# Norms split over three engines, a reordered head, a store in parts, and a quarter of the gate rows on ScalarE, in a two-layer kernel

## The chip, the cores and the metric
The kernel runs on one core of a Trainium2 chip. The metric is the device time of one execution in microseconds; the median of the runs is compared. Five engines matter here: TensorE (PE in the rows; PEld is its weight load), VectorE (DVE), ScalarE (ACT), GpSimd (POOL) and SyncE (SP), whose queue issues most of the DMAs.

## The reference, cut to what matters
Two transformer-like layers over 256 tokens of width 1024, everything in float32. Layer one:

```python
mod = silu(c) @ w_ada + b_ada                    # 6 x 1024 values: shift, scale, gate, twice
xn = rms_norm(h, norm1_g) * (1.0 + sc1) + sh1
proj = xn @ w_in                                 # q, k, v of 8 heads; RWKV inputs; gate logits
mixed = g_moba * (attention @ w_proj_moba) + g_rwkv * (rwkv @ w_proj_rwkv)
h = h + gt1 * (mixed @ w_out)
xn2 = rms_norm(h, norm2_g) * (1.0 + sc2) + sh2
h = h + gt2 * peer_ffn(xn2, ...)                 # q = xn2 @ wq, top 16 of 16384 experts per head
```

`rms_norm` is x * rsqrt(mean(x*x) + eps) * gain over the 1024 features. `peer_ffn` chooses for each token and each of 8 heads 16 of 128 x 128 experts, takes gelu(xn2 . u) times the softmaxed score, and sums the experts' v rows. The second layer is of the same shape: norm, `w_in_2`, two attentions, `w_o`; then norm, `w_up`, a causal convolution of width 3, silu gate, `w_down`:

```python
x = x + gate_a * ((g_a * o_a + g_b * o_b) @ w_o)
h = rms_norm_2(x, ffn_norm) * (1.0 + scale_f) + shift_f
x = x + gate_f * ((silu(gt) * val) @ w_down)
```

So there are four norms over the residual, each between two matrix products.

## The kernel before, in words
Activations lie transposed: 128 partitions hold features, and a tile `hT[:, m, :]` is 128 features of all 256 tokens; the residual is 8 such tiles. Weights come as tiles of 128 x 1024 (512 KB) through a ring `wring` of six slots. SyncE issues them in order, each as soon as the tile six earlier is done (`tile_done`). Most products are computed in three TensorE passes of a split: ScalarE writes the rounded upper part of a tile to `whi` (L455, three slots), VectorE the rest to `wlo` (L460), and `three` (L463) multiplies upper by upper, upper by rest and rest by upper. The phases "w_in", "wq", "peer", "w_in2" and "ffn" are split so; "proj", "w_out" and "w_o" multiply float32 directly, and each such float32 matmul stands in the trace as two records.

Each engine has its own list of work, written out by hand at the end of the kernel (from L2329); semaphores alone tie them together. There is no planner.

The norm (L503 to L537) is a relay in which each step handles all eight tiles: `norm_squares` (VectorE, one operation on 2048 columns), `norm_pe` (eight matmuls with ones into bank 3), `norm_act` (square root on ScalarE), `norm_scale` (reciprocal, and the product of all tiles with it, VectorE), `norm_shift` (eight operations on VectorE with the modulation's scale and shift), `x_upper` (eight casts on ScalarE) and `x_rest` (four subtractions on VectorE). TensorE begins when all of `xn` is there (L835, L1813) or all of the split (L1451, L2200).

The head: SyncE loads the silu input `crow`, four tiles of `ada` (512 KB each), then columns, constants, x and positions, then twelve more `ada` tiles, each waiting for a free slot of four, then six weight tiles. VectorE forms one dot product per `ada` tile (L822, 128 x 1024); sixteen are needed for the first norm: eight scales and eight shifts. TensorE computes the first four tiles of w_in, the values with tokens on partitions, one tile after another: for each tile and token half eight matmuls with 128 columns (`matmul8_tokens`, L488). After that come the split tiles, beside which VectorE runs eight more dot products, and the position angles (`dve_trig`, L896) run ahead of all splits.

The gate rows (`dve_hot` L1584, `pe_gates` L1600, `act_gates` L1613): for 64 groups of four tokens VectorE builds one-hot rows, A4 (one operation for four tokens, L1589) and B4 (one operation per token, one-hot times the gate weight, L1591); TensorE multiplies them, four tokens into one bank, and one matmul of an early expert tile stands between groups (L1611); ScalarE copies the bank to `G` and, once in eight groups, takes the Gelu of an early expert tile.

After the experts the sum lies with tokens on partitions; TensorE turns it back (L1687) and VectorE adds it to the residual (L1794). At the end `dve_add_accs` (L1801) waits for the last tile, adds all eight accumulators, and SyncE stores the result with one DMA (L2323).

Of the kernel before, what the change touches and what calls it, by code (L numbers as in the profile page):

```python
# [15 lines left out]
P = 128  # L16
# [154 lines left out]
def build_layer_pair(nc, a):  # L171

    with ExitStack() as ctx:
# [65 lines left out]
        aring = rA["aring"].rearrange("p (s n) -> p s n", s=ASLOTS)  # L239
        zraw = arena[:, 3584:3584 + 14 * 257].rearrange("p (m t) -> p m t", m=14)  # L240
# [25 lines left out]
        rB, _ = region(arena, 32256, [("crow", D), ("aring", BSLOTS * D)])  # L266
# [6 lines left out]
        rG, _ = region(arena, S * NK + 2 * KT * S, [("T3", 768), ("A4", 1024), ("B4", 1024)])  # L273
        rG.update(region(arena, AFTER_WHI, [("ge", 768), ("crow2", D), ("iota", 128)])[0])
        rG.update(region(arena, AFTER_WHI + 768, [("iotai", 128)])[0])
# [98 lines left out]
        def ring_tiles(pe, name, body):  # L374
# [23 lines left out]
            for k in range(n, count):  # L398
                one(slot_of(first + k), (ring0 + k) % BANKS, count_at(first + k), ring0 + k - BANKS + 1)

# [102 lines left out]
        def norm_pe(pe, n, sq):  # L503
            pe.wait_ge(sq_ready, n + 1)
            for k in range(KT):
                mm = pe.matmul(bank[3][:, 0:S], ones, sq[:, k, :], start=(k == 0), stop=(k == KT - 1))
            mm.then_inc(ss_ready, 1)

        def norm_act(act, n, rt):
            act.wait_ge(ss_ready, n + 1)  # L510
            act.activation(rt, bank[3][:, 0:S], ACT.Sqrt, scale=1.0 / D, bias=col("eps")).then_inc(rt_ready, 1)

        def norm_squares(dve, sq):
            dve.tensor_tensor(sq[:, :, :], hT[:, :, :], hT[:, :, :], ALU.mult).then_inc(sq_ready, 1)

        def norm_scale(dve, v, n, rt):
            dve.wait_ge(rt_ready, n + 1)
            v.then(dve.reciprocal(rt, rt))
            v.then(dve.tensor_tensor(xn[:, :, :], hT[:, :, :], over(rt, KT), ALU.mult))

        def norm_shift(dve, n, shift):
# [4 lines left out]
        def x_upper(act, n):  # L526

            for k in range(KT):
                act.wait_ge(xn_ready, KT * n + k + 1)
                act.copy(xhi[:, k, :], xn[:, k, :]).then_inc(x_hi, 1)  # L530

        def x_rest(eng, n):

            for k in range(0, KT, 2):
                eng.wait_ge(x_hi, KT * n + k + 2)
                eng.tensor_tensor(xlo[:, k:k + 2, :], xn[:, k:k + 2, :], xboth[:, k:k + 2, 0, :].bitcast(F32),
                                  ALU.subtract).then_inc(x_lo, 1)  # L537

# [160 lines left out]
        def sp_loads(sp):  # L699
            for dst, src in ((cols[:, :], a["cols"]), (keep[:, :], a["keep"]), (hT[:, :, :], a["xT"]),  # L700
                             (posi, a["positions"].to_broadcast([P, S]))):
                sp.dma_start(dst, src).then_inc(loaded, 16)

        def sp_ada(sp):

            sp.dma_start(crow, a["crow"][0:1, :].to_broadcast([P, D])).then_inc(crow_loaded, 16)
            for t in range(2 * KT):
                if t == ASLOTS:
                    sp_loads(sp)
                if t >= ASLOTS:  # L710
                    sp.wait_ge(ada_used, t - ASLOTS + 1)
                sp.dma_start(aring[:, t % ASLOTS, :], a["ada"][t]).then_inc(alanded[t % ASLOTS], 16)

        def sp_w_in(sp):
# [9 lines left out]
            for t in range(SLOTS):  # L724
                sp.dma_start(wring[:, t, :], a["w"][t]).then_inc(landed[t], 16)
            sp.dma_start(r0["const1"], a["const1"][:, 0:NC1]).then_inc(c1_loaded, 16)
            sp.dma_start(rA["select1"], a["const1"][:, NC1:NC1 + NS1]).then_inc(c1_loaded, 16)
# [8 lines left out]
        dots_before = lambda j: min(max(3 * j // 2, 0), 3 * KT)  # L736
# [81 lines left out]
        def dve_ada(dve, n):  # L818

            dve.wait_ge(alanded[n % ASLOTS], 16 * (n // ASLOTS + 1))  # L820
            src = aring[:, n % ASLOTS, :]
            dve.tensor_tensor_reduce(src, src, crow, 1.0, 0.0, ALU.mult, ALU.add, mod[:, n:n + 1]).then_inc(ada_used, 1)  # L822

# [10 lines left out]
        def pe_w_in(pe):  # L834
            pe.wait_ge(xn_ready, KT)  # L835
# [21 lines left out]
        def act_w_in_tile(act, t):  # L857

            if t + 2 >= SKIP["w_in"]:
                act_hi_of(act, "w_in", t + 2)  # L860
            tile_wait(act, "w_in", t)
            bk = bank[t % BANKS]
            if t < 4:
# [1679 lines left out]
```

## Time and profile before

| what | us |
|---|---|
| median of 3 runs | 1910.35 (1909.63 to 1910.8) |
| profiled execution | 1909.39 |
| its span, first to last instruction | 1907.6 |
| TensorE busy | 1731.3 (91%) |
| VectorE busy | 1337.7 (70%) |
| ScalarE busy | 728.6 (38%) |
| GpSimd busy | 98.9 (5%) |
| granted TensorE clock, mean | 0.962 of full |
| chain of waits: TensorE, VectorE | 77%, 17% |

Busy time is the union of an engine's instructions. The chain of waits is followed back from the last instruction; a share in it is time on which the end depends. 316 MB move, 166 GB/s as a mean over the span.

### The profile page before, as it was taken

To read this page: it belongs to the slowest core of one execution; us is meant where nothing else is said; L and a number is where in the kernel's file an instruction comes from. 1 tells how busy PE (TensorE), PEld (TensorE's weight loads), DVE (VectorE), ACT (ScalarE), POOL (GpSimd) and SP (SyncE) were. 2 spreads that over 40 slices of the span, in tenths; PEclk is the share of its full clock that TensorE was granted. 3 is DMA by queue.
4 is the path that set the end of the run, shared out by engine and by line. 5 is a ranking of instruction groups with operands and counts; after the bars stand their busy time and mean duration, and the time that the engine had idled before them with its cause. 6 is when DMAs were issued, how large, how long until landed. Compare 5 with 4: busy or idle time off the path is not lost.

```text
span 1907.6 us, 30181 instructions
## 1 busy us (share of the span) xinstructions
PE 1731.3 (91%) x10370; PEld 1503.9 (79%) x10370; DVE 1337.7 (70%) x2720; ACT 728.6 (38%) x1275; POOL 98.9 (5%) x107
## 2 busy tenths in 40 slices
PE   2987999969997989999999999999799988879997
PEld 2986888759885767788888888887798846669997
DVE  7678553763999977688888888887445545448886
ACT  1443101113212344455555555554244215324443
POOL 0022000000000000000000000000007103200000
PEclk8999999989998989999999999999899988989999
DMA  9642003655561127677777777777355460035553
GB/s 332 233 136 69 23 16 108 216 216 165 159 189 46 56 81 242 211 234 240 233 237 235 236 239 234 239 234 222 110 181 152 125 209 1 23 96 180 182 181 110
DMA packets 101311, 316.24 MB, mean 166 GB/s; under 512 B 11248, under 2 KB 20464, under 8 KB 100720
## 3 DMA queue, kind: packets, MB, share of 16 engines
q1 hardware_dynamic: 100512, 311.07, 51.2%
q10 hardware_dynamic: 720, 4.11, 0.6%
q8 instruction: 50, 0.82, 0.2%
q14 instruction: 29, 0.24, 0.0%
HBM read 309.63 MB, written 5.51 MB: 165 GB/s over the span
## 4 chain that ended last, share of the span: by engine, by line
PE 77%; DVE 17%; DMA 2%; issue 2%; POOL 1%; ACT 1%; SPq 0%; ACTq 0%; DVEq 0%; POOLq 0%
PE bank L481 8%; PE bank L466 7%; PE bank L467 7%; PE bank L468 7%; PE bank L1647 6%; PE bank L1649 6%; PE bank L1651 6%; PE bank L482 4%; PE bank L1606 4%; PE bank L442 3%; PE bank L492 2%; PE bank L1398 2%; PE bank L582 1%; PE bank L1496 1%; PE bank L485 1%
## 5 line engine op out<-in xcount | busy, mean ns | idle before, releaser
L460 DVE TENSOR_TENSOR wlo<-wring,whi 128x1024 fp32r<-128x1024 f32 x348 | 423.9, 1224 | 114.5 <-ACT whi L455 106.7
L455 ACT CAST whi<-wring 128x1024 fp32r<-128x1024 f32 x364 | 380.9, 1048 | 73.5 <-PE bank L1651 49.1
L466 PE MATMUL bank<-xboth,whi 128*128 128x256 f32 x960 | 276.3, 288 | 25.5 <-DVE wlo L460 23.3
L467 PE MATMUL bank<-xboth,whi 128*128 128x256 f32 x960 | 273.3, 285 | 0.0
L468 PE MATMUL bank<-xboth,wlo 128*128 128x256 f32 x960 | 273.2, 285 | 0.0
L481 PE MATMUL bank<-xboth,whi 128*128 128x512 f32 x658 | 235.8, 397 | 0.0
L466 PEld LDWEIGHTS bank<-xboth,whi 128*128 128x128 f32 x960 | 186.0, 194 | 28.9 <-issue 24.4
L467 PEld LDWEIGHTS bank<-xboth,whi 128*128 128x128 f32 x960 | 186.1, 194 | 0.6 <-issue 0.5
L468 PEld LDWEIGHTS bank<-xboth,wlo 128*128 128x128 f32 x960 | 185.9, 194 | 0.0
L482 PE MATMUL bank<-xboth,wlo 128*128 128x256 f32 x658 | 184.5, 280 | 0.0
L1647 PE MATMUL bank<-whi,Whi 128*128 128x512 f32 x512 | 161.0, 396 | 14.9 <-DVE Wlo L1742 14.9
L1649 PE MATMUL bank<-wlo,Whi 128*128 128x512 f32 x512 | 159.9, 394 | 0.0
L1651 PE MATMUL bank<-whi,Wlo 128*128 128x512 f32 x512 | 159.0, 392 | 0.0
L481 PEld LDWEIGHTS bank<-xboth,whi 128*128 128x128 f32 x658 | 123.6, 188 | 29.4
L1496 PE MATMUL bank<-xn,wring 128*128 128x256 f32 x544 | 128.6, 380 | 0.0
L482 PEld LDWEIGHTS bank<-xboth,wlo 128*128 128x128 f32 x658 | 124.2, 189 | 3.7
L1647 PEld LDWEIGHTS bank<-whi,Whi 128*128 128x128 f32 x512 | 97.3, 191 | 33.4 <-issue 9.8
L1649 PEld LDWEIGHTS bank<-wlo,Whi 128*128 128x128 f32 x512 | 97.2, 190 | 21.5
L1651 PEld LDWEIGHTS bank<-whi,Wlo 128*128 128x128 f32 x512 | 97.0, 189 | 21.4
L1496 PEld LDWEIGHTS bank<-xn,wring 128*128 128x128 f32 x544 | 98.6, 191 | 10.7
L1751 DVE TENSOR_TENSOR arena<-arena 128x256 f32<-128x256 f32 x94 | 59.8, 636 | 56.0 <-ACT arena L1710 56.0
L460 POOL TENSOR_TENSOR wlo<-wring,whi 128x1024 fp32r<-128x1024 f32 x16 | 45.7, 2862 | 1016.4 <-ACT whi L455 1016.4
(367 smaller groups left out, 2893.5 us busy)
## 6 DMA issues: line engine op xcount, KB each, us to landing
wring<-in_w SPq DMA_DIRECT2D x463, 512.0 KB, 3.9
arena<-in_ada SPq DMA_DIRECT2D x48, 512.0 KB, 5.6
xn<-in_ada SPq DMA_DIRECT2D x96, 256.0 KB, 3.3
h_spill<-arena SPq DMA_DIRECT2D x34, 128.0 KB, 1.7
arena<-h_spill SPq DMA_DIRECT2D x34, 128.0 KB, 3.5
wring<-in_w SPq DMA_DIRECT2D x6, 384.0 KB, 3.1
wring<-in_w SPq DMA_DIRECT2D x9, 256.0 KB, 2.6
arena<-in_const ACTq DMA_DIRECT2D x1, 1200.0 KB, 5.3
```

What stands on the lines that cost most here:

```text
L455: act.copy(whi[:, n % HSLOTS, :], wring[:, n % SLOTS, :]).then_inc(hi_ready, 1)
L460: eng.tensor_tensor(wlo[:, n % SLOTS, :], wring[:, n % SLOTS, :], whi[:, n % HSLOTS, :].bitcast(F32), ALU.subtract).then_inc(lo_ready, 1)
L466: pe.matmul(out, h, xh, start=start, stop=False, **kw)
L467: pe.matmul(out, h, xl, start=False, stop=False, **kw)
L468: return pe.matmul(out, l, xh, start=False, stop=stop, **kw)
L481: pe.matmul(out, h, xboth[:, k, :, :], start=(k == 0), stop=False)
L482: pe.matmul(out[:, 0:S], l, xhi[:, k, :], start=False, stop=False)
L1496: mm = pe.matmul(bank[j % 3][:, 0:S], blocks(n % SLOTS, k), xn[:, k, :], start=(k == 0), stop=(k == KT - 1))
L1606: mm = pe.matmul(bank[3 + n % 4][:, t * 128:(t + 1) * 128], A4[:, n % 2, t, :], B4[:, n % 2, t, :], start=True, stop=True)
L1647: pe.matmul(tok_accs[b][f][:, :], Wh, h[:, f * 512:(f + 1) * 512], start=first, stop=False)
L1649: pe.matmul(tok_accs[b][f][:, :], Wh, l[:, f * 512:(f + 1) * 512], start=False, stop=False)
L1651: mm = pe.matmul(tok_accs[b][f][:, :], Wl, h[:, f * 512:(f + 1) * 512], start=False, stop=last)
```

## The change
1. Norms. Squares go to ScalarE, a tile at a time; the ones-matmul of a tile follows in TensorE's list two tiles behind the product that made it (in w_out and w_o). The sum lies in bank 4. After the reciprocal VectorE scales tile by tile, ScalarE shifts (Identity with scale and bias from columns) and casts, and VectorE subtracts pairs of tiles. TensorE waits for rows or pairs of rows: `split_pair` runs the first two weight tiles of wq and of ffn together, over k outside. Those two tiles are split before the norm ends (beside the residual).
2. Head. A ring of sixteen slots; scale and shift tiles come in pairs of the same feature tile; SyncE issues everything without waiting, weight tiles among them. The four value tiles are computed together, k outside, 512 columns a matmul. The angles' operations stand between the splits of tiles 6, 7 and 8.
3. Dot products beside proj and w_out are spread by a table (DOTS). `crow` of that stage lies elsewhere.
4. Gate rows. VectorE builds three of the four B4 rows; ScalarE the fourth, as Relu(gate - gate * (id - iota)^2), in two operations.
5. End. The last down tile signals each pair of accumulators; adds and store follow in four parts.
6. Semaphores of the head norms of the attentions are merged into one family (`head_*`), with counts carried on; nothing in the order of those operations changes.

```diff
+        hring = arena[:, 7680:7680 + 2 * KT * D].rearrange("p (t n) -> p t n", t=2 * KT)
...
-        def matmul8_tokens(pe, bk, slot, width=128):
+        def matmul8_tokens(pe, bk, slot, norm=None, width=128):
             for b in range(TT):
                 for k in range(KT):
+                    if norm is not None and b == 0:
+                        pe.wait_ge(xn_ready, KT * norm + k + 1)
...
+        def act_square(act, n, m, sq):
+            act.activation(sq[:, m, :], hT[:, m, :], ACT.Square).then_inc(sq_ready, 1)
+        def norm_sum(pe, n, m, sq):
+            pe.wait_ge(sq_ready, KT * n + m + 1)
+            mm = pe.matmul(bank[NORM_BANK][:, 0:S], ones, sq[:, m, :], start=(m == 0), stop=(m == KT - 1))
...
+        def norm_scale(dve, rt):
             for k in range(KT):
-                dve.tensor_scalar(xn[:, k, :], xn[:, k, :], gsc[:, n, k:k + 1], modc(shift, k),
-                                  ALU.mult, ALU.add).then_inc(xn_ready, 1)
+                dve.tensor_tensor(xn[:, k, :], hT[:, k, :], rt, ALU.mult).then_inc(x_scaled, 1)
+        def norm_shift(act, n, k, shift):
+            act.wait_ge(x_scaled, KT * n + k + 1)
+            act.activation(xn[:, k, :], xn[:, k, :], ACT.Identity, scale=gsc[:, n, k:k + 1],
+                           bias=modc(shift, k)).then_inc(xn_ready, 1)
...
+        def norm_shift_split(act, n, shift):
+            norm_shift(act, n, 0, shift)
+            for k in range(1, KT):
+                norm_shift(act, n, k, shift)
+                x_upper(act, n, k - 1)
+            x_upper(act, n, KT - 1)
...
+        def split_pair(pe, outs, n, norm):
+            for k in range(KT):
+                if k % 2 == 0:
+                    pe.wait_ge(x_lo, 4 * norm + k // 2 + 1)
+                for i in range(2):
+                    mm = three(pe, outs[i], n + i, k, xhi[:, k, :], xlo[:, k, :], k == 0 and (i == 0 or outs[2]),
+                               k == KT - 1, skip_group_check=True)
...
+            sp.dma_start(crow, a["crow"][0:1, :].to_broadcast([P, D])).then_inc(crow_loaded, 16)
+            pair(0)
+            for dst, src in ((hT[:, :, :], a["xT"]), (keep[:, :], a["keep"]), (cols[:, :], a["cols"]),
                              (posi, a["positions"].to_broadcast([P, S]))):
                 sp.dma_start(dst, src).then_inc(loaded, 16)
+            pair(1)
+            pair(2)
+            for t in range(4):
+                tile(t)
+            for k in range(3, KT - 1):
+                pair(k)
+            tile(4)
+            pair(KT - 1)
+            tile(5)
...
-        dots_before = lambda j: min(max(3 * j // 2, 0), 3 * KT)
+        DOTS = (0, 1, 3, 4, 6, 7, 9, 10, 12, 13, 15, 17, 19, 21, 23, 24, 24)
...
+        def dve_head(dve, v):
...
+            dots(0)
+            dots(1)
+            dve.wait_ge(loaded, 64)
+            norm_root(dve, v, 0, rtn[0])
+            dve.tensor_tensor(xn[:, :, :], hT[:, :, :], over(rtn[0], KT), ALU.mult)
+            known(0, 2)
+            dots(2)
+            dots(3)
+            known(2, 4)
+            dots(4)
+            dots(5)
+            known(4, 6)
+            x_rest_pair(dve, 0, 0)
+            dots(6)
+            known(6, 7)
+            x_rest_pair(dve, 0, 2)
+            dots(7)
+            known(7, 8)
+            x_rest_pair(dve, 0, 4)
+            x_rest_pair(dve, 0, 6)
...
         def pe_w_in(pe):
             for t in range(4):
                 pe.wait_ge(landed[t], 16)
-                if t >= BANKS:
-                    pe.wait_ge(ring_free, t - BANKS + 1)
-                matmul8_tokens(pe, bank[t % BANKS], t).then_inc(tile_done, 1)
+            for k in range(KT):
+                pe.wait_ge(xn_ready, k + 1)
+                for b in range(TT):
+                    mm = pe.matmul(bank[5 + b][:, :], xn[:, k, b * 128:(b + 1) * 128],
+                                   wring[:, 0:4, k * 128:(k + 1) * 128], start=(k == 0), stop=(k == KT - 1))
+            mm.then_inc(tile_done, 4)
...
+            ring_tiles(pe, "w_out", lambda slot, bk: matmul8(pe, bk[:, 0:S], slot, mix1),
+                       after=lambda k: k >= 2 and norm_sum(pe, 1, k - 2, nsq[1]))
+            for m in (KT - 2, KT - 1):
+                norm_sum(pe, 1, m, nsq[1])
+        def act_w_out(act):
+            w = FIRST["wq"]
+            for m in range(KT):
+                act.wait_ge(ring_free, RING0["w_out"] + m + 1)
+                act_square(act, 1, m, nsq[1])
+                if m in (5, 6):
+                    act_hi(act, w + m - 5, count_at(w + m - 5), None)
...
-                for t in range(4):
+                for t in range(3):
                     ins = dve.tensor_scalar(B4[:, b, t, :], rG["iota"], T3[:, 1, t0 + t:t0 + t + 1],
                                             T3[:, 2, t0 + t:t0 + t + 1], ALU.is_equal, ALU.mult)
...
+        def act_hot(act, n):
+            t, away = 4 * n + 3, rG["away"][:, (n % 2) * 128:(n % 2) * 128 + 128]
+            if n >= 2:
+                act.wait_ge(hot_act, n - 1)
+            act.activation(away, rG["iota"], ACT.Square, scale=-1.0, bias=T3[:, 1, t:t + 1]).then_inc(away_ready, 1)
+            act.wait_ge(away_ready, n + 1)
+            act.activation(B4[:, n % 2, 3, :], away, ACT.Relu, scale=rG["ngate"][:, t:t + 1],
+                           bias=T3[:, 2, t:t + 1]).then_inc(hot_act, 1)
         def act_gates(act):
+            act.wait_ge(t3_ready, 1)
+            act_hot(act, 0)
+            act_hot(act, 1)
             for n in range(GROUPS):
                 act.wait_ge(g_ready, n + 1)
                 act.copy(G[:, 4 * n:4 * n + 4, :], bank[3 + n % 4][:, :].rearrange("p (t j) -> p t j", t=4))\
                    .then_inc(g_copied, 1)
+                if n + 2 < GROUPS:
+                    act_hot(act, n + 2)
...
         def sp_out(sp):
-            sp.wait_ge(acc_read, 2)
-            sp.dma_start(a["out"], hT[:, :, :]).then_inc(stored, 16)
-            sp.wait_ge(stored, 16)
+            for m in range(0, KT, 2):
+                sp.wait_ge(acc_read, KT + m + 2)
+                sp.dma_start(a["out"][:, m:m + 2, :], hT[:, m:m + 2, :]).then_inc(stored, 16)
+            sp.wait_ge(stored, 16 * (KT // 2))
```

## Rows read from the trace of the kernel before

**Rows 1.** Stretches: us, busy of PE, PEld, DVE, ACT, POOL, clock, DMA share, GB/s
```profile
29.70:41.20 11.50, 0.00 (x0) 0.00 (x0) 11.33 (x21) 2.26 (x8) 0.00 (x0) 0.50 0.98 358
...
1703.00:1708.00 5.00, 4.68 (x24) 4.71 (x25) 2.44 (x3) 0.00 (x0) 0.00 (x0) 0.55 0.01 3
```
**Rows 2.** Chain of waits at the head: start us, length us, what
```profile
5.12 10.15 DMA arena<-in_positions
...
41.22 16.45 PE bank L492 x128
```
**Rows 3.** Groups of instructions by shape: names, shapes, count, busy us, mean ns
```profile
L460 DVE TENSOR_TENSOR wlo<-wring,whi 128x1024 fp32r<-128x1024 f32 x348 | 423.9, 1224 | 114.5 <-ACT whi L455 106.7 <-issue 7.1
L455 ACT CAST whi<-wring 128x1024 fp32r<-128x1024 f32 x364 | 380.9, 1048 | 73.5 <-PE bank L1651 49.1 <-PE bank L468 17.8
...
L442 PE MATMUL bank<-arena,wring 128*128 128x256 f32 x256 | 57.7, 388 | 8.6 <-DVE arena L2093 7.4 <-DVE arena L1411 1.2
...
L822 DVE CUSTOM_DVE_ANT_0 arena<-arena 128x1024 f32<-128x1024 f32 x24 | 28.8, 1222 | 9.1 <-DMA arena<-in_ada 8.8
...
L626 ACT ACTIVATE arena<-arena 128x256 f32<-128x256 f32 x32 | 15.9, 496 | 0.0
...
L626 ACT ACTIVATE arena<-arena 128x128 f32<-128x128 f32 x32 | 12.9, 403 | 2.2 <-DVE arena L657 1.6
...
L530 ACT CAST xboth<-xn 128x256 fp32r<-128x256 f32 x32 | 10.7, 405 | 29.1 <-DVE xn L523 29.1
...
L1965 PE MATMUL bank<-arena 128*128 128x512 f32 x14 | 6.2, 592 | 0.0
```
**Rows 4.** Timeline at the norm after w_out: start us, us, instruction
```profile
407.75 0.48 DVE L1430 SCALAR_TENSOR_TENSOR hT<-bank,mod,hT 128x256 f32<-128x256 f32 x1 [1.83 <-PE bank L442]
...
419.31 1.75 DVE L518 RECIPROCAL arena<-arena 128x256 f32<-128x256 f32 x1 [6.29 <-ACT arena L511]
...
423.87 2.67 ACT L530 CAST xboth<-xn 128x256 fp32r<-128x256 f32 x8 [4.66 <-DVE xn L523]
426.00 2.50 DVE L536 TENSOR_TENSOR xboth<-xn,xboth 128x512 fp32r<-128x512 f32 x4
...
429.78 0.58 PE L466 MATMUL bank<-xboth,whi 128*128 128x256 f32 x1 [11.08 <-DVE wlo L460]
```
**Rows 5.** Timeline at the norm after the experts
```profile
1333.87 2.82 DVE L1794 SCALAR_TENSOR_TENSOR hT<-bank,mod,hT 128x256 f32<-128x256 f32 x7
...
1337.10 1.28 ACT L511 ACT_TABLE_LOAD   x1 [4.67 <-DVE hT L1794]
...
1351.75 4.47 PE L492 MATMUL bank<-wring,xn 128*128 128x128 f32 x20 [7.39 <-DVE xn L523]
```
**Rows 6.** Timeline at the norm after w_o
```profile
1685.69 0.48 DVE L1430 SCALAR_TENSOR_TENSOR hT<-bank,mod,hT 128x256 f32<-128x256 f32 x1 [2.97 <-PE bank L442]
...
1703.32 0.55 PE L466 MATMUL bank<-xboth,whi 128*128 128x256 f32 x1 [11.04 <-DVE wlo L460]
...
1715.71 0.42 DVE L2308 TENSOR_TENSOR Wlo<-arena,Whi 128x256 fp32r<-128x256 f32 x1
```
**Rows 7.** Timeline of one group of gate rows
```profile
650.34 0.85 DVE L1589 TENSOR_TENSOR arena<-arena 128x512 f32<-128x512 f32 x1
...
650.64 1.16 PE L1606 MATMUL bank<-arena 128*128 128x128 f32 x8
650.94 1.27 DVE L1591 TENSOR_SCALAR arena<-arena 128x128 f32<-128x128 f32 x4
...
651.64 0.60 PE L1496 MATMUL bank<-xn,wring 128*128 128x256 f32 x2
651.84 0.59 ACT L1616 COPY arena<-bank 128x512 f32<-128x512 f32 x1 [1.04 <-PE bank L1606]
...
652.27 1.16 PE L1606 MATMUL bank<-arena 128*128 128x128 f32 x8
```
**Rows 8.** Timeline of the end
```profile
1900.01 3.23 DVE L1803 SCALAR_TENSOR_TENSOR hT<-bank,mod,hT 128x256 f32<-128x256 f32 x8 [4.69 <-PE bank L468]
```

More of the change, by code:

```diff
@@ L500, in ring_bank @@
             return bank[(RING0[name] + k) % BANKS]
[L503 to L507, printed above, removed]
+        x_scaled = sem("x_scaled")
+        NORM_BANK = 4
+        def act_square(act, n, m, sq):
[3 more added lines that the diff above has]
+            mm = pe.matmul(bank[NORM_BANK][:, 0:S], ones, sq[:, m, :], start=(m == 0), stop=(m == KT - 1))
+            if m == KT - 1:
+                mm.then_inc(ss_ready, 1)
@@ L818, in dve_ada, with dots, known @@
         def dve_ada(dve, n):
-            dve.wait_ge(alanded[n % ASLOTS], 16 * (n // ASLOTS + 1))
+            dve.wait_ge(alanded[n % ASLOTS], ada_count(n))
             src = aring[:, n % ASLOTS, :]
             dve.tensor_tensor_reduce(src, src, crow, 1.0, 0.0, ALU.mult, ALU.add, mod[:, n:n + 1]).then_inc(ada_used, 1)
+        def dve_head(dve, v):
+            def dots(k):
+                dve.wait_ge(pair_landed[k], 32)
+                for vec in range(2):
+                    src = hring[:, 2 * k + vec, :]
+                    dve.tensor_tensor_reduce(src, src, crow, 1.0, 0.0, ALU.mult, ALU.add,
+                                             modc(vec, k)).then_inc(ada_used, 1)
+            def known(k0, k1):
+                two = mod[:, 0:2 * KT].rearrange("p (v m) -> p v m", v=2)[:, :, k0:k1]
+                bias = col("b_ada", 0, 2 * KT).rearrange("p (v m) -> p v m", v=2)[:, :, k0:k1]
+                dve.wait_ge(ada_used, 2 * k1)
+                v.then(dve.tensor_tensor(two, two, bias, ALU.add))
+                dve.scalar_tensor_tensor(gsc[:, 0, k0:k1], modc(1, k0, k1 - k0), 1.0, col("norm1_g", k0, k1 - k0),
+                                         ALU.add, ALU.mult).then_inc(x_scaled, k1 - k0)
+            dve.wait_ge(crow_ready, 1)
+            dots(0)
[18 more added lines that the diff above has]
+            x_rest_pair(dve, 0, 6)
         def dve_add_bias(dve, v, lo_m, hi_m):
@@ L871, in act_w_in @@
         def act_w_in(act):
-            for t in range(ATT_TILE - 3):
+            for n in (4, 5):
+                act_hi(act, n, 16, None)
+            act.wait_ge(tile_done, 4)
+            for b in range(TT):
+                act.copy(vtok[:, b, :], bank[5 + b][:, :]).then_inc(ring_free, 2)
+            for t in range(4, ATT_TILE - 3):
                 act_w_in_tile(act, t)
@@ L1465, in act_route @@
             act_subk(act)
-            for t in range(2):
-                act_hi_of(act, "wq", t)
+            act.wait_ge(ada_used, 6 * KT)
             for t in range(COUNT["wq"]):
@@ L1636, in down8 @@
                            skip_group_check=True)
+                if last and m % 2:
+                    mm.then_inc(acc_done, 1)
             return mm
@@ L1690, in pe_peer @@
                     mm.then_inc(tok_turned, 1)
+            for m in range(KT):
+                norm_sum(pe, 2, m, nsq[2])
         def act_peer(act):
@@ L1732, in act_peer @@
             ins.then_inc(tok_ready, 1)
+            for m in range(KT):
+                act.wait_ge(acc_read, m + 1)
+                act_square(act, 2, m, nsq[2])
         def dve_peer(dve, v):
@@ L2190, in pe_w_o, with act_w_o @@
             pe.wait_ge(mix_ready, 1)
-            ring_tiles(pe, "w_o", lambda slot, bk: matmul8(pe, bk[:, 0:S], slot, oA))
+            ring_tiles(pe, "w_o", lambda slot, bk: matmul8(pe, bk[:, 0:S], slot, oA),
+                       after=lambda k: k >= 2 and norm_sum(pe, 3, k - 2, nsq[3]))
+            for m in (KT - 2, KT - 1):
+                norm_sum(pe, 3, m, nsq[3])
+        def act_w_o(act):
+            act.wait_ge(mix_ready, 1)
+            for m in range(KT):
+                act.wait_ge(ring_free, RING0["w_o"] + m + 1)
+                act_square(act, 3, m, nsq[3])
+                if m in (5, 6):
+                    act_hi(act, F0 + m - 5, count_at(F0 + m - 5), None)
         f_z, f_u, f_g, f_whi, f_w = sem("f_z"), sem("f_u"), sem("f_g"), sem("f_whi"), sem("f_w")
@@ L2213, in down @@
                 pe.wait_ge(f_w, 2 * i + (f + 1))
-                down8(pe, n, f % 2, first, last).then_inc(tile_done, 1)
-            up(0, 0)
+                mm = down8(pe, n, f % 2, first, last)
+                if not last:
+                    mm.then_inc(tile_done, 1)
+            up_first()
             up(1, 0)
@@ L2250, in turn @@
                 silu(f, i)
-            for n in range(F0, F0 + 4):
+            for n in range(F0 + 2, F0 + 4):
                 hi(n, 0)
@@ L2343, in _ @@
         def _(pe):
-            norm_pe(pe, 0, sq0)
+            for m in range(KT):
+                norm_sum(pe, 0, m, sq0)
             pe_w_in(pe)
@@ L2363, in _ @@
             act_head(act)
+            act.wait_ge(loaded, 64)
+            for m in range(KT):
+                act_square(act, 0, m, sq0)
             norm_act(act, 0, rtn[0])
-            x_upper(act, 0)
+            norm_shift_split(act, 0, 0)
             act_w_in(act)
```

299 lines of the change are left out of this document (153 added, 146 removed).

## The prediction

> **What bounds the kernel now.** I read the busy shares first: TensorE is busy nearly everywhere and holds most of the chain of waits, so only three things can pay: TensorE's idle holes, fewer TensorE cycles, and stretches where TensorE is paced by another engine. The table of stretches then shows a hole at the head: in 29.7 to 41.2 us TensorE does nothing, while the DMA engines are at 0.98 [rows 1]. The chain shows why the hole ends where it does: the first load batch (4.2 MB up to the positions) lands at 15.3, dot products on VectorE follow, and then 64 small matmuls (128 records) of value tiles take 16.45 us, so the split tiles start at 57.7 [rows 2]. The timeline shows the same kind of hole at each later norm: 407.75 to 429.78 [rows 4], the last residual of the experts to 1351.75 [rows 5], 1685.69 to 1703.32 [rows 6]. In the gate-row stage VectorE sets the pace: its groups and with them TensorE's start every 1.62 us (650.64, 652.27), and the first operation of each starts right behind the last of the one before [rows 7]. At the end eight adds and one store stand alone [rows 8].
>
> Every sum below is made against the profiled execution, 1909.39 us, 0.96 under the median 1910.35.
>
> **Head.** All sixteen scale and shift tiles, the constants and six weight tiles are now asked for without waiting. What must land before the last pair of scale/shift tiles: 8.39 MB of them, 0.52 crow, 1.05 hT, 0.55 small constants, 2.62 of weights, 13.1 MB. 4.2 MB landed at 15.3. Rate after that: 358 GB/s is the mean of a stretch at 0.98 [rows 1]; a queue never empty should do a little better, I take 385 (an estimate; its ends are 358 and a seventh more, 410). (13.1-4.2)/0.385 = 23.2, so the last pair lands at 38.5. Then on the path: two dots of 1.22 (row of L822 [rows 3]), 0.1, bias and gain 0.45: 41.4. Shift on ScalarE: a one-operand ACTIVATE of 128x256 takes 0.496 where a cast without one takes 0.405; the shift has two such operands, 0.59 [rows 3]: 42.0. x_upper, the split of tile 4 (1.05 and 1.23, a cast and L460's 1224 ns [rows 3]) come to 45.0; the last value matmuls (four records of 6.2/14 = 0.443 us, L1965 [rows 3]) are done at 43.8. So the split tiles start at 45.0, not 57.7: -12.7. The value tiles' own work falls from 16.45 to 32 x 0.443 = 14.2 and lies mostly under the loads, so it isn't counted again. Cover that is lost: the trig chain (4 us of VectorE) lay under the value tiles; now it sits between splits of tiles 6 to 8, where VectorE needs 1.23+1.22 per tile anyway against 2.88 (24 matmuls of 0.12) of TensorE. It overruns by 0.8, 1.3 and 0.5, partly met by a lead of one tile: +1.8. TensorE has gaps of 1 to 2 us between its row pairs and may fall to the lower of its two clock levels (after a long idle it ran at 0.55 for 5 us [rows 1]): +0.9. Head: -10. Bounds: -5 (358 GB/s, low clock for two pairs) to -14.
>
> **Norm after w_out.** Squares move to ScalarE and the eight ones-matmuls between tiles. Six of them lengthen w_out by 6 x 0.43 = 2.6 (two records of L442's 57.7/256 [rows 3]). Last tile done at 410.35; residual 0.48, square 0.41, sum 0.45. The square root's table load (1.28, L511 [rows 5]) used to run while ScalarE was idle; now it comes behind the last square and ends 0.8 after the sum: 412.55. Root 0.5, reciprocal 1.75 [rows 4], first scaling 0.42: 415.3. ScalarE alternates shift and cast: casts start 0.32 apart (8 in 2.67 [rows 4]), shifts 0.5, so the second cast is out at +2.2; the first subtraction (0.69 of the four in 2.50 [rows 4]) at +3.0, and TensorE begins at 418.3, row pair by row pair. It needs 1.44 us per pair at full clock, ScalarE makes one in 1.64; at the lower clock of the first 5 us TensorE needs 2.6, so it is not starved. The first two tiles' splits are done inside w_out, where VectorE has 0.5 us or more free per tile because the dot products there are spread to two per tile and none in the last. 429.78-418.3: -11.5. Bounds -9 and -12.8 (root table hidden, no clock or pacing loss). Third tile's split: ready 1 to 2 us before it is needed.
>
> **Gate rows.** VectorE per group: A4 0.60 (650.34 to 650.94), the four row operations the other 1.02; three of them 0.77: 1.37 [rows 7]. TensorE per group: eight records in 1.00 (650.64 to 651.64) and the early expert's pair, 0.43: 1.43. ScalarE: copy, Square, Relu. Copy 0.586 [rows 7]; a 128x128 ACTIVATE with one operand 0.403, the Relu with two 0.49 [rows 3]; each starts 0.09 before its predecessor ends (casts of 0.405 start 0.32 apart [rows 4]), except behind its own wait, 0.04: 0.49+0.40+0.04+0.40 = 1.33. So three engines lie at 1.33 to 1.43; TensorE leads. I take 1.45: 62 x 0.17 = 10.5, less 0.4 for the negated gate row ahead: -10. Queued behind the Square's wait on ScalarE are the copies that free the banks; four banks give them slack of two groups. Bounds: -15 (VectorE's 1.37 rules) and +4 (rival A).
>
> The row for a table load says 1.283 us and in this trace copies and casts never bring one [rows 5]. Square, Identity and Relu have no row. The Trainium skill, ScalarE: Activation LUTs, "Table sets: the hidden batching unit", has relu, copy and identity as filler of every set; it doesn't say so of Square, and it budgets about 2.7 us per switch, twice the row. By it Relu and Identity are free of loads and Square stays open.
>
> VectorE does a one-hot row in 0.25, ScalarE in 0.84 [rows 3, 7]: moving it pays only while ScalarE idles. The skill's rule on the same page ("Rules for kernel authors") is to keep relu, add and mul on VectorE; by it every moved operation would cost time. Here it bites only when ScalarE's 1.33 passes TensorE's 1.43, and that is rival A's condition.
>
> **Norm after the experts.** Residual row by row, squares and sums follow it: last residual 1336.69, square 1337.15, issue of the constants' DMA 0.34, table 1.28, root 0.5, reciprocal 1.75, scaling 0.42, shift 0.59: 1342.1 against 1351.75. The first token tile waits per row; shifts come every 0.5 against 0.43 for a row of matmuls at the low clock: +0.3. -9.4. Bounds -7.5, -10.5.
>
> **Norm after w_o.** The same as after w_out: from the last tile's end to TensorE 7.95 us. 1685.69+2.6+7.95 = 1696.25 against 1703.32 [rows 6]: -7.1. Late next is the first down tile: W was ready at 1716.1 [rows 6], half a us before TensorE; it hangs on both first tiles being done, which now end together: +0.6. -6.5. Bounds -5, -8.
>
> **End.** Adds follow each pair of accumulators, so two of eight remain behind TensorE: 3.23-0.85 = 2.4 less. The store of 1 MB fills the rest, from the adds' end at 1903.24 [rows 8] to 1907.6, 4.3 us; the last quarter should take 2.5: -1.8. -4.2. Bounds -2.5, -5.
>
> Semaphores that are merged count the same events in the same order: 0.
>
> **Sum.** 10+11.5+10+9.4+6.5+4.2 = 51.6. 1909.4-51.6 = 1857.8, as a median 1858.7; I say 1858.
>
> **Rivals.**
> A, ScalarE bounds the gate rows. If Gelu and Square lie in different tables, the eight early Gelus of the stage bring 16 loads, 20.5 us; 64 x 1.33+20.5 = 106 against about 100 now: +4 instead of -10: 1872. For: no row shows Gelu and Square sharing a table. Against: copies and casts live with every table. 0.10.
> B, VectorE keeps the gate rows at 1.37: 62 x 0.25-0.4 = 15: 1853. For: 1.37 and 1.43 are close, and the pair's 0.43 is read from another line. Against: 1.43 is made of TensorE's own starts. 0.14.
> C, the relays cost more than added. Loads at 358 GB/s (+1.7), low clock on the last value pairs and the first split tile (+2.5), 1 us more in each of three norms for handovers: +7: 1865. For: every hand-over is a semaphore, and gaps of 2 us can cost clock. 0.19.
> D, slower than before. Square and Relu lie in tables that exclude each other, so each group brings two loads: 64 x (1.33+2.57) = 250 us in place of 100: 1858+160 = 2018. It decides as soon as the stage loses the 42 us that the rest gains, which is 0.7 load per group. Against: the same as in A, twice over. 0.02.
>
> **From this to the numbers.** Forecast 0.53, A 0.10, B 0.14, C 0.19, D 0.02; the last 0.02 is for a loss that I don't see, half of it to each of no change and slower. Faster 0.96, same 0.01, slower 0.03; 0.2% (4 us) is what a measurement here can tell. The range takes the bounds of head and norms, and B and most of C, and leaves A and D out: 1847 to 1870.
>
> **What would show it.** TensorE's first split matmul near 45; norm holes of about 10.6, 5.4 and 10.6 us in place of 22.0, 15.1 and 17.6 (from last tile or residual to first matmul); gate groups every 1.45 us, no table load in them beyond the first; first value matmul near 22, in bursts; store ending 2.5 us after the last add. Wrong it is if a Square brings a load, if ScalarE is busy through the gate rows, if tile 7 or 8 of w_in waits over 3 us for its split, or if the last pair lands after 41.

## The result, and the profile after

The changed kernel takes 1850.95 us (median of 4 runs, 1849.70 to 1852.73); the kernel before took 1910.57 in the runs beside it (4 runs, 1909.63 to 1912.66). The ratio is 0.9687, 95% interval 0.967 to 0.9704. Forecast was 1858, range 1847 to 1870. The profiled execution took 1849.88 (span 1848.1) against 1909.39: 59.5 us less, where 51.6 were forecast.

Busy shares, from the page after: TensorE's share grows (91% before) though it is busy for less time in all (1712.4 us against 1731.3), since its holes are smaller.

```profile
PE 1712.4 (93%) x10274; PEld 1489.9 (81%) x10274; DVE 1304.4 (71%) x2650; ACT 800.3 (43%) x1465; POOL 96.8 (5%) x107
```

To see where 59.5 us came from, I followed TensorE's first instruction of each stage through both traces; a stage's gain is the growth of the lead. The gate rows are counted from TensorE's six transposes ahead of them (586.28 before, 566.03 after) to their last record.

| stretch | forecast | measured |
|---|---|---|
| head, to the sums for the query and key norms (83.50 to 74.45) | -10 | -9.1 |
| rest of layer 1's mixers | 0 | +1.4 |
| w_out and the norm after it, low clock behind it | -11.5 | -12.6 |
| gate rows | -10 | -15.3 |
| experts | 0 | +0.65 |
| norm after the experts | -9.4 | -9.7 |
| layer 2's attention, to w_o | 0 | -3.5 |
| norm after w_o, to the last down tile | -6.5 | -6.1 |
| end | -4.2 | -5.15 |

**Head.** The chain of waits after (start, length, what) and two rows of the table of stretches (columns as in [rows 1]):

```profile
3.93 9.25 DMA arena<-in_positions
...
38.13 1.13 DVE arena L883
39.27 1.14 DVE arena L883
...
40.84 0.61 ACT xn L536
41.49 2.00 PE bank L932 x4
43.51 6.02 DMA wring<-in_w
```
```profile
36.00:40.00 4.00, 4.00 (x11) 1.61 (x9) 3.93 (x8) 0.90 (x2) 0.00 (x0) 1.00 0.77 311
40.00:44.00 4.00, 2.34 (x5) 0.68 (x4) 3.01 (x7) 3.16 (x6) 0.00 (x0) 1.00 0.68 210
```

Where one load and 128 value records stood [rows 2], VectorE's dot products now make the chain; TensorE is full beside them and only four value records (2.00) are left behind the last. The last line of the chain is a weight load that is asked for when the value tiles are done (43.51) and lands at 49.5: the chain goes on through the waits of the split tiles. The first split matmul starts at 44.56 (before 57.42; the 57.67 of [rows 2] is the end of the value matmuls, which the split ones overlap).

**Norm after w_out**, timeline after, answering to [rows 4]:

```profile
402.22 0.48 DVE L1549 SCALAR_TENSOR_TENSOR hT<-bank,mod,hT 128x256 f32<-128x256 f32 x1 [1.12 <-PE bank L447]
402.74 0.42 ACT L514 ACTIVATE arena<-hT 128x256 f32<-128x256 f32 x1 [2.53 <-DVE hT L1549]
...
403.17 1.28 ACT L524 ACT_TABLE_LOAD   x1
403.21 0.70 PE L518 MATMUL bank<-arena,keep 128*128 128x256 f32 x2 [0.16 <-ACT arena L514]
404.47 0.47 ACT L524 ACTIVATE arena<-bank,cols 128x256 f32<-128x256 f32 x1
404.97 1.75 DVE L528 RECIPROCAL arena<-arena 128x256 f32<-128x256 f32 x1 [0.59 <-ACT arena L524]
...
409.44 0.69 DVE L562 TENSOR_TENSOR xboth<-xn,xboth 128x512 fp32r<-128x512 f32 x1
...
410.28 0.55 PE L471 MATMUL bank<-xboth,whi 128*128 128x256 f32 x1 [6.37 <-DVE xboth L562]
```

From the last residual to TensorE it takes 8.06 us instead of 22.03. The square and the sum are short; the table load ends after the sum, and the reciprocal is the longest piece.

**Norms after the experts and after w_o**, timeline after, answering to [rows 5, 6]: after the experts it takes 8.6 us from the first residual to the first token matmul (before 18.3, the first residual there at 1333.47). After w_o it is 8.06 again (before 17.63), and there is a new wait of 1.66 at the first down tile.

```profile
1298.55 3.23 DVE L1940 SCALAR_TENSOR_TENSOR hT<-bank,mod,hT 128x256 f32<-128x256 f32 x8 [0.76 <-PE bank L1828]
...
1302.24 1.28 ACT L524 ACT_TABLE_LOAD   x1
...
1307.11 1.20 PE L499 MATMUL bank<-wring,xn 128*128 128x128 f32 x4 [3.83 <-ACT xn L536]
```
```profile
1639.50 0.48 DVE L1549 SCALAR_TENSOR_TENSOR hT<-bank,mod,hT 128x256 f32<-128x256 f32 x1 [2.27 <-PE bank L447]
...
1647.56 0.55 PE L471 MATMUL bank<-xboth,whi 128*128 128x256 f32 x1 [6.37 <-DVE xboth L562]
...
1662.98 0.39 PE L471 MATMUL bank<-Whi,whi 128*128 128x256 f32 x1 [1.66 <-DVE wlo L465]
```

**Gate rows.** One group in the timeline after, answering to [rows 7]. VectorE's first operation starts at 643.68 and again at 645.06; the median distance is 1.37, and between the two VectorE is never idle. ScalarE has next to nothing free either (95% busy from the first group to the last): copy, Square, Relu, copy. No table load is among them: ScalarE's last one before the stage stands at 537.6, for Gelu, and the next at 663.1.

```profile
643.68 0.59 ACT L1753 COPY arena<-bank 128x512 f32<-128x512 f32 x1
643.68 0.69 DVE L1711 TENSOR_TENSOR arena<-arena 128x512 f32<-128x512 f32 x1
...
644.16 0.40 ACT L1742 ACTIVATE arena<-arena 128x128 f32<-128x128 f32 x1
644.29 0.85 DVE L1713 TENSOR_SCALAR arena<-arena 128x128 f32<-128x128 f32 x3
644.60 0.49 ACT L1744 ACTIVATE arena<-arena 128x128 f32<-128x128 f32 x1
...
645.00 0.59 ACT L1753 COPY arena<-bank 128x512 f32<-128x512 f32 x1
645.06 0.69 DVE L1711 TENSOR_TENSOR arena<-arena 128x512 f32<-128x512 f32 x1
```

**End**, timeline after, answering to [rows 8]: the adds begin 1.8 us before TensorE's last matmul (1843.93), and the stores are asked for from the second add on.

```profile
1842.10 3.23 DVE L1952 SCALAR_TENSOR_TENSOR hT<-bank,mod,hT 128x256 f32<-128x256 f32 x8 [1.13 <-PE bank L473]
1843.00 2.68 SPq L2482 DMA_DIRECT2D out_hT<-hT  x4
```

### The profile page after: what moved, and what is told of

Same layout as the page of the kernel before. It is cut to its first block, busy times and chain, and to the rows that moved or that the text cites. A ratio compares the mean times of both kernels' runs of the same rounds, so it can differ in the third digit from the quotient of the medians.

```text
span 1848.1 us, 30116 instructions
## 1 busy us (share of the span) xinstructions
PE 1712.4 (93%) x10274; PEld 1489.9 (81%) x10274; DVE 1304.4 (71%) x2650; ACT 800.3 (43%) x1465; POOL 96.8 (5%) x107
## 4 chain that ended last, share of the span: by engine, by line
PE 77%; DVE 17%; DMA 2%; issue 2%; ACT 2%; POOL 1%; SPq 0%; DVEq 0%; ACTq 0%; POOLq 0%
PE bank L486 8%; PE bank L471 7%; PE bank L472 6%; PE bank L473 6%; PE bank L1788 6%; PE bank L1790 6%; PE bank L1792 6%; PE bank L487 4%; PE bank L1729 3%; PE bank L447 3%; PE bank L1506 2%; PE bank L1617 2%; PE bank L622 1%; PE bank L490 1%; PE bank L2122 1%
```

## The experiments

Each edit is against the changed kernel. The kernels ran in three groups, and the kernel before stood at 1906.9, 1912.3 and 1908.8 in them, so effects under about 5 us are read from the traces. g_act0, g_pe and h_dots leave out part of the work. No run undoes the new norms one by one: their gains stand in the timelines above alone.

### Gate rows: which engine holds a group

```diff
 # g_dve4 (also g_act0 and g_pe, with the loop below)
-                for t in range(3):
+                for t in range(4):
                     ins = dve.tensor_scalar(B4[:, b, t, :], ...)
-                pe.wait_ge(hot_act, n + 1)
-            act_hot(act, 0); act_hot(act, 1); ... act_hot(act, n + 2)
 # g_act0: 3, g_pe: 2
+                for t in range(4 if n < 2 else 3):
 # g_two: act_hot makes rows 2 and 3, its two Squares first, then its two Relus
+                for t in range(2):
```


> Undoes the gate-row part alone: all four one-hot rows of a group on VectorE, nothing of them on ScalarE. If the gain of that stage (measured 15.3 us, forecast 10) is the part's own, a group starts every 1.62 us again and the time is 15 us above the changed kernel, 1866. If part of the 15.3 came from elsewhere (granted clock, earlier loads), it is 10 above, 1861, with a group every 1.54.

> Leaves out ScalarE's row from the third group on (the fourth row of a group keeps old contents), VectorE still makes three. In the changed kernel VectorE, TensorE and ScalarE all stand at 1.37 us a group. If ScalarE is what holds the stage, the group falls below 1.37 to at most TensorE's 1.35 and the stage gains 1 us or more; if VectorE or TensorE holds it, the time stays within 0.5 us of the changed kernel, 1851, and ScalarE's rows are shown to be hidden.

> Leaves out two rows of four: VectorE makes two (1.12 us a group), ScalarE none, the others keep old contents. What is left is TensorE's own pace. By my forecast (1.43 of TensorE: eight records in 1.00, a pair in 0.43) nothing changes beyond noise. By the theory that VectorE's 1.37 holds the stage and TensorE has slack, the group falls to 1.12 to 1.3 and the stage loses 5 to 16 us: 1835 to 1846.

> Two rows a group on ScalarE and two on VectorE. VectorE 1.12 us a group; ScalarE 0.49 for the copy, two Squares and two Relus at 0.36 to 0.49 each: 2.2 us. If the rival 'ScalarE bounds the stage' decides as soon as ScalarE has more than 1.37, the group is 2.2 us and the kernel 50 us slower than the changed one, 1904. If Square or Relu waited only for each other (latency, not rate) and two in flight overlap, it is 1.8 us and 1879.

| kernel | rows VectorE / ScalarE | first to last group, us | group, us | median, us |
|---|---|---|---|---|
| changed | 3 / 1 | 88.56 | 1.37 | 1850.95 |
| g_dve4 | 4 / 0 | 104.14 | 1.63 | 1864.51 |
| g_act0 | 3 / 0 | 88.55 | 1.37 | 1851.48 |
| g_pe | 2 / 0 | 84.94 | 1.32 | 1850.19 |
| g_two | 2 / 2 | 117.86 | 1.83 | 1881.53 |

The part is worth 15.6 us in the traces (104.14 to 88.56). ScalarE's row is hidden, busy as that engine is: without it the stage takes the same 88.55. With VectorE's work cut to 1.12 a group falls only to 1.32. The timeline of g_pe shows why: TensorE starts eight records, the early expert's pair and the next eight with no gap, 0.89 + 0.44 = 1.33. That is its own pace. In the kernel before [rows 7] the eight records took 1.00, and there TensorE waited 0.2 for VectorE before each group: the second record of a group starts 0.21 after the first (median of 55 groups, 0.11 in g_pe), and every later one 0.11 after the one before it.

```profile
640.53 1.05 PE L1728 MATMUL bank<-arena 128*128 128x128 f32 x8
...
641.42 0.60 PE L1617 MATMUL bank<-xn,wring 128*128 128x256 f32 x2
...
641.86 1.05 PE L1728 MATMUL bank<-arena 128*128 128x128 f32 x8
```

So VectorE's 1.37 holds the changed stage, TensorE is 0.04 behind it, and 3.6 us is all that more relief could bring. g_pe's median did not show it: its trace lost 4 us elsewhere (below). In g_two ScalarE holds it, and the timeline has it without a gap:

```profile
641.19 0.67 ACT L1756 COPY arena<-bank 128x512 f32<-128x512 f32 x1
...
641.65 0.80 ACT L1743 ACTIVATE arena<-arena 128x128 f32<-128x128 f32 x2
642.25 0.98 ACT L1747 ACTIVATE arena<-arena 128x128 f32<-128x128 f32 x2
...
643.02 0.67 ACT L1756 COPY arena<-bank 128x512 f32<-128x512 f32 x1
```

A second row costs 0.46 us, not the 0.83 of my first expectation: two Squares together leave out the wait that a Square and its Relu have between them (the Relu of the changed kernel starts at 644.60, 0.04 after its Square ends). The second alternative, 1879, was near (1881.53). One row on ScalarE is the right share; two are worse than none by 13.7 us in the stage (117.86 against 104.14). The medians differ by 17.0, but 4.2 of the 17.3 between these two traces lie in layer 2's attention, where neither kernel was edited (below).

### Head: the angle chain, early loads, VectorE or the loads

```diff
h_trig:
 dots(0)
+dve.wait_ge(loaded, 64)
+dve_trig_turns(dve, v)
+dve_trig_angle(dve, v)
+dve_trig_args(dve, v)
 dots(1)
-dve.wait_ge(loaded, 64)
 norm_root(dve, v, 0, rtn[0])
... (the three dve_trig calls are gone from the splits of tiles 6 to 8)
```


> The eleven operations of the angle chain on VectorE move from the splits of tiles 6 to 8 of w_in into the head, ahead of the dot products of the second pair, where VectorE idles from 10.2 to 16.0 us (constants land near 13). My theory: they cost nothing there (VectorE is next needed at 19.7, when the root is out) and tiles 7 to 9 no longer wait for their splits: 2.6 us less, 1848.4. Rival: the wait of tiles 7 to 9 is for weights still landing (DMA share 1.0 up to 60 us), so taking VectorE's work away only uncovers that: under 0.5 us.

Median 1844.57 (5 runs), ratio 0.9648 [0.963, 0.9666]. In the timeline the chain runs from 13.28, and the dot products of the second pair still end before the root:

```profile
13.28 0.29 DVE L996 CAST arena<-arena 128x256 f32<-128x256 int32 x1 [3.05 <-DMA arena<-in_positions]
...
17.35 1.22 DVE L883 CUSTOM_DVE_ANT_0 arena<-arena 128x1024 f32<-128x1024 f32 x1
18.50 1.22 DVE L883 CUSTOM_DVE_ANT_0 arena<-arena 128x1024 f32<-128x1024 f32 x1
19.79 0.47 ACT L524 ACTIVATE arena<-bank,cols 128x256 f32<-128x256 f32 x1 [2.65 <-PE bank L518]
```

From the first split matmul to the sums TensorE took 26.5 us. The head's code is the same in seven other kernels here (the changed one, the four of the gate rows, n_table, e_end): there it took 27.7 to 29.9, mean 28.4. So the chain costs 1.9 us where it stood (2.6 were expected), and the rest of the median's 6.4 is not its own.

```diff
h_ada (the first four ada tiles behind the head):
+for k in range(4):
+    sp.wait_ge(ada_used, 2 * k + 2)
+    n = 2 * KT + k
+    sp.dma_start(aring[:, n % ASLOTS, :], a["ada"][n]).then_inc(alanded[n % ASLOTS], 16)
 sp.wait_ge(ada_used, 2 * KT)
 ...
-for k in range(2):
-    ada(2 * KT + k)
 for k in range(4, COUNT["w_in"]):
 ...
-    if k + 2 < KT + 4:
+    if k + 2 < KT + 4 and k >= 6:
         ada(2 * KT + k - 2)
```


> The first four scale/shift tiles that follow the head are asked for as soon as their slots are free, not in turn with the weight tiles, so that they land in the hole of 38 to 44 us where the DMA share is 0.7. My theory: the waits of split tiles 5 and 6 (0.30 and 0.83 us, for a tile that lands at 45.5 and a weight tile that lands at 49.5) go: 1.1 to 1.7 us less, 1849.5. Rival: they push the last pair of the head back (queue full to 38 us) and the first split matmul comes later than 44.6: 0 to 3 us more.

Median 1850.25, ratio 0.9672 [0.9651, 0.9692]. First split matmul 45.55, sums at 73.22, against 45.0 and 73.4 (means of the seven): a tile's wait saved, half a us lost, nothing gained. The rival was right in part.

```diff
h_dots:
-dots(4)
+for vec in range(2):
+    dve.wait_ge(pair_landed[4], 32)
+    dve.memset(modc(vec, 4), 0.0).then_inc(ada_used, 1)
```


> Leaves out the two dot products of the fifth scale/shift pair (their two columns are set to zero), all loads as in the changed kernel. My forecast had the landing of the last pair (38.5) hold the head; by that, with the loads unchanged, the first split matmul stays at 44.6. The theory that VectorE holds it (busy without a gap from 24.0 to 41.3 us, while the loads end by 39.5) gives 2.3 us earlier, 42.3, and 1.5 to 2.5 us off the time, as the weights of tile 6 are then also asked for earlier.

Median 1843.17, but the head did not move: first split matmul 44.47, sums 73.54. VectorE, freed of 2.4 us, waits for the sixth pair:

```profile
31.32 1.22 DVE L883 CUSTOM_DVE_ANT_0 arena<-arena 128x1024 f32<-128x1024 f32 x1 [1.98 <-DMA arena<-in_ada]
...
40.75 0.60 ACT L536 ACTIVATE xn<-xn,mod,gsc 128x256 f32<-128x256 f32 x1 [2.39 <-DVE gsc L891]
```

In the changed kernel VectorE came to that pair at 31.41, and it lands at 31.32. My theory of VectorE alone fell: the loads hold the head until 31.3, and from there six dot products and two subtractions without a wait, to 40.7, are VectorE's. By little: the last pair landed at 37.72 in the changed kernel and VectorE came to it at 38.05; in the seven traces it came 0.3 to 1.2 us after the landing. Both are at their limit at once, and less work on VectorE alone can bring no more than that at the last pair. Most of the 7.8 us of its median comes from the stretch after the sums (below), with the head's end where it was.

### Root table, and a version with all of it

```diff
n_table:
+def act_prefetch(act):
+    act.activation(probe[:, 0:1], col("eps"), ACT.Sqrt)
... (called after the square of row 4 at w_out and w_o, and ahead of the first after the experts)
```


> A square root of one column is put on ScalarE after the fifth square of the norms after w_out and w_o, and before the first square of the norm after the experts. If Square lives beside the square root's table, the load (1.28 us) is then hidden and the real root waits for TensorE's sum alone: 0.8 + 0.3 + 0.8 = 1.9 us less, 1849. Rival: Square brings its own table back, so the load stays where it was and one more comes in each norm, most of it between tiles: 0 to 2.5 us more.

Median 1848.08, ratio 0.9668 [0.9655, 0.9682]. The load sits between tiles and Square brings none back, so the rival is out:

```profile
388.45 1.28 ACT L514 ACT_TABLE_LOAD   x1
...
399.67 0.42 ACT L519 ACTIVATE arena<-hT 128x256 f32<-128x256 f32 x1 [2.53 <-DVE hT L1556]
400.88 0.47 ACT L529 ACTIVATE arena<-bank,cols 128x256 f32<-128x256 f32 x1 [0.79 <-PE bank L523]
```

Last residual to TensorE falls from 8.06 to 7.54 at both tile norms, first residual to root from 4.99 to 4.76 at the experts: 1.3 us in all, not 1.9, since the root now waits 0.79 for TensorE's sum.

> The three edits together: angle chain early, four scale/shift tiles early, root table early. If each is on the path by itself, the gains add: 5.6 to 6.2 us less than the changed kernel, 1845. If the angle chain and the late loads hide each other, the two together give more than their sum, up to 2 us more.

Median 1843.49, ratio 0.9654 [0.9635, 0.9672]; sums at 70.74, 26.1 us after the first split matmul (nine tiles of 24 matmuls at 0.12 are 25.9), so no tile of the head waits any more. The three edits are worth 2.6 (73.35 to 70.74) + 1.3 = 3.9 us in the traces, less than the 5.6 to 6.2 expected: each of the three had brought less than its own expectation. The interval barely meets the changed kernel's.

```diff
best: both, and
-x_rest_pair(dve, 0, 0)
-x_rest_pair(dve, 0, 2)
+x_rest_pair(pool, 0, 0); x_rest_pair(pool, 0, 2)    # on GpSimd
```


> The three edits of 'both', and the first two row pairs of the head's split of x (0.68 us each) on GpSimd, which idles, in place of VectorE. If VectorE holds the head, the first split matmul comes 1.2 us earlier than in 'both' (44.7), near 43.4, and the time is 1 us less, 0.9 to 1.2 us under 'both'. Rival: GpSimd takes 1.4 us for each and slows VectorE's dot products beside it; then nothing is gained or 1 us lost.

Median 1848.66: the rival was right. In the timeline a dot product that starts beside GpSimd's subtraction takes 2.29 instead of 1.22 (2.30 beside the first of the two), and the first split matmul comes at 45.22 and the sums at 71.30, 0.56 after those of `both`. The medians of `both` and `best` differ by 5.2 and their traces by 2.3; what is over 0.56 is not traced to this edit.

```profile
36.04 1.27 POOL L567 TENSOR_TENSOR xboth<-xn,xboth 128x512 fp32r<-128x512 f32 x1 [4.85 <-ACT xboth L547]
...
36.09 2.29 DVE L890 CUSTOM_DVE_ANT_0 arena<-arena 128x1024 f32<-128x1024 f32 x1
```

The dot product is longer by 1.07, nearly all that was left of GpSimd's operation. The Trainium skill, SBUF — State Buffer, "Who interferes with whom", says that a VectorE instruction with two SBUF inputs contends with a GpSimd instruction that reads SBUF, and that this contention is an exclusive lock; the trace agrees, with those 1.07 us.

### End

```diff
e_end:
-    if m % 2 == 0: dve.wait_ge(acc_done, m // 2 + 1)
+    if m == 0:     dve.wait_ge(acc_done, 4)
...
-for m in range(0, KT, 2): (a store of two rows each)
+sp.wait_ge(acc_read, 2 * KT)
+sp.dma_start(a["out"][:, :, :], hT[:, :, :]).then_inc(stored, 16)
```


> Undoes the end alone: the eight adds wait for all accumulators, and one store of 1 MB follows them. By the terms of the forecast 4.2 us more (2.4 adds, 1.8 store), 1855. If 1.5 us of the 5.15 measured at the end were TensorE's clock in its last 24 matmuls and not the code, it is 3.6 us more and the last matmuls run at full clock here too.

Median 1854.28, ratio 0.9727 [0.971, 0.9743].

```profile
1842.04 3.23 DVE L1952 SCALAR_TENSOR_TENSOR hT<-bank,mod,hT 128x256 f32<-128x256 f32 x8 [3.29 <-PE bank L473]
1845.30 0.35 SPq L2481 DMA_DIRECT2D out_hT<-hT  x1
```

From the start of the last matmul to the end of the span: 7.87 here (1841.73 to 1849.6), 4.17 in the changed kernel (1843.93 to 1848.1), 7.91 before. The code is worth 3.7. The other 1.4 of the measured 5.15 is clock: the last 24 matmuls start over 2.83 us in both kernels of this pair, and over 4.23 in the kernel before. Both traces of the kernel before have that low clock there (4.23 and 4.26) and none of the twelve others (2.82 to 2.83), e_end among them; what sets it off is not shown.

### What moves without an edit

> The kernel before once more, for a second trace. In the stretch from the norm after the experts to w_o the traces so far take 300.6 us or 304.7, with the same code. If that is the chip's and not the change's, this trace can show 300.6 for the kernel before too (its first showed 304.1); if the kernel before always has it, 304.1 again.

One execution, 1913.42. Its rows for layer 2's attention, and the same columns of two kernels that there have the same code, `both` and `h_trig`:

```profile
1575.00:1580.00 5.00, 1.44 (x16) 0.66 (x8) 3.51 (x7) 0.00 (x0) 0.00 (x0) 0.50 0.00 0
1590.00:1595.00 5.00, 5.00 (x16) 3.55 (x15) 2.10 (x14) 2.15 (x9) 1.06 (x3) 0.50 0.01 3
```
```profile
1510.00:1515.00 5.00, 3.11 (x26) 1.27 (x26) 1.57 (x3) 1.76 (x2) 0.00 (x0) 0.50 0.10 39
1530.00:1535.00 5.00, 5.00 (x16) 3.44 (x16) 1.23 (x8) 2.31 (x10) 1.30 (x4) 0.50 0.00 0
```
```profile
1510.00:1515.00 5.00, 2.38 (x23) 1.58 (x24) 1.90 (x9) 1.79 (x3) 0.00 (x0) 1.00 0.76 244
1530.00:1535.00 5.00, 3.81 (x18) 2.62 (x19) 2.67 (x21) 3.82 (x17) 2.25 (x6) 0.84 0.00 0
```

In this stretch, where TensorE is half idle, the granted clock falls to 0.50 (`before2`: the first fence). In `both` it stays there for some 25 us (1510 to 1535), in `h_trig` for 10, and the matmuls of 1530 to 1535 run at 0.50 or at 0.84. From the first token matmul to w_o that makes two lengths: 300.3 to 300.9 us in eight traces of the changed kernel and its kin, 304.6 to 304.9 in three (g_pe, g_two, both), 303.2 in best. The kernel before had 304.1 and 304.8. So the same code gives either, and the 3.5 us of the table can be that alone, since the change edits nothing there but the names and counts of semaphores. But both traces of the kernel before were long, so my expectation that it too can be short stays unshown, and with it that none of the 3.5 is the change's. From the sums to w_out it is likewise 296.3 and 296.7 before, 297.7 in the changed kernel, 296.3 to 297.2 in eight of its kin, 294.9 in two and 292.0 in h_dots. The +1.4 of the table is within that, and it explains most of h_dots's median.

## Why the prediction was right, step by step

The time lies in the stated range by the holes, which came out as added up; one term, the gate rows, was mis-sized by a third, and 3.5 us came from a stage that I had put at nothing: that was luck.

**What bounds it, and the order of the holes:** right. Nothing but the named holes and the gate rows moved by more than the spread between traces told above.

**Head, -10 (measured -9.1).** First split matmul at 45.0 forecast; 44.56 here, 45.0 the mean of the seven traces. It was to come from 57.7; it came from 57.42. The last pair landed at 37.72 (38.5 forecast), since the queue ran at 410 GB/s, the upper end of my estimate. But VectorE, whose row of dot products I had not added up, came to the pair 0.33 us after it had landed; from there to the first split matmul it took 6.51, as forecast (6.5). So the landing was not the last cause, and the mean of 45.0 is in part luck: in the seven traces a landing earlier than forecast and VectorE's 0.3 to 1.2 us behind it cancel. Given back behind it: 1.8 forecast for the angle chain; h_trig measures 1.9. The whole that is given back is 4.0 in this trace and 2.5 in the mean of seven; the rest is waits for loads that I had not costed. The head's mean is then 73.4 against 83.6, -10.2.

**Norm after w_out, -11.5 (-12.6).** Hole 7.95 forecast, 8.06 measured (the sign of 10.6 counts the 2.6 by which w_out was to grow). w_out grew by 2.16, not 2.6: five sums stand before the last tile, not six. The rest is the low clock behind the hole, 2.8 us of it instead of 4.5, worth about 0.8, which I had counted as unchanged.

**Gate rows, -10 (-15.3).** This term was mis-sized, and rival B, at 0.14, is what happened. The step that failed: "TensorE per group: eight records in 1.00 ... and the early expert's pair, 0.43: 1.43". The 1.00 was the distance from the first record to the pair in a trace where TensorE had waited for VectorE before the first record, and the second started 0.1 us late; its own eight records take 0.89 (g_pe), and eight and a pair 1.33. VectorE's 1.37 was exact and so held the stage; ScalarE's 1.33 is close to what it has in the trace. My sign of being wrong, ScalarE busy through the gate rows, came true (95%), and g_act0 shows that it was no sign: ScalarE was busy and held nothing.
Rival A needed Gelu and Square in different tables: no load came. On my doubt about Square: it brought no load in any trace here, neither behind Gelu nor behind a root. Rival D falls with it.

**Norm after the experts, -9.4 (-9.7).** Right: last residual to first matmul 5.3 us, 5.4 forecast, and the root's load ends after the last sum.

**Norm after w_o, -6.5 (-6.1).** -7.5 at TensorE, 1.4 given back at the first down tile. I had named the tile, with 0.6, for W. W's last part is ready at 1661.79, about half a us after TensorE is free, as I had it; what I missed is the split of the tile's weights, which stands behind W in VectorE's list and ends at 1662.92 (the 1.66 in the row at 1662.98).

**End, -4.2 (-5.15).** 3.7 by e_end, plus 1.4 of clock. Of the 3.7 the adds bring 2.1 (2.4 forecast) and the store 1.6 (1.8): it ends 2.75 us after the last add, not 2.5.

**Rival C,** relays dearer than added: no. The three holes came out within 0.1 us of the sum; that the semaphores' hand-overs were in the pitches that I took from [rows 4] is my reading, and no run separates them.

The first value matmul came at 24.93, not near 22; nothing hangs on it, as TensorE was done with all but the last row when that row came (41.49).

In all 7.9 us more than forecast: 5.3 from the gate rows, 3.5 from layer 2's attention, where the clock was low for a shorter time, and the rest cancels.

## What to carry to other kernels

Read an engine's own pace from records that wait for nothing: here the first record behind a wait took 0.21 us to the second instead of 0.11, and those 0.1 us a group hid a third of a stage's gain. When three engines are brought to within 0.1 us of each other the stage is done, and one row more on the slower engine (ScalarE makes in 0.9 what VectorE makes in 0.25) turned a gain of 15.6 us in the stage into a loss of 13.7 against none. A kernel with idle stretches of TensorE carries a few us of granted clock that differ from execution to execution; follow the starts of stages through several traces before a difference of that size is given to an edit.

## Not expected of the hardware

A VectorE dot product of 128x1024 took 2.29 us instead of 1.22 beside a GpSimd subtraction of 1.27. In one stretch with holes in TensorE's work the clock stayed at half for 10 or for 25 us with the same code, worth 4 us. Loads of 512 KB that were queued without waits ran at 410 GB/s (15 to 31 us of the changed kernel), where the kernel before, with a wait for a slot ahead of each, had 358 [rows 1]. The first matmul record of a gate group was followed by the next one after 0.21 us where TensorE had waited 0.2 us before it (kernel before), and after 0.11 where it had not (g_pe).
